# One transfer per weight tile in place of two half transfers, in a four-layer model on one core

## The chip, the core and the metric

The kernel runs on one core of a Trainium2 chip. The metric is the device time of one execution in microseconds (us). The core has a matrix engine (TensorE, PE in the profile, with its weight loads as PEld), three engines for elementwise work (VectorE or DVE, ScalarE or ACT, GpSimd or POOL), a queue engine (SyncE or SP) that here only issues transfers, and 16 DMA engines between the off-chip memory and the on-chip buffer.

## What is computed

Four layers on 512 tokens of width 1024, in float32: a dilated-window attention, a differential attention, then a block with a recurrent mixer, a cross attention to a memory of 256 rows and a squared-ReLU network, and a block with a sliding-window attention, again a cross attention and a squared-ReLU network. Every one is a chain of matrix products with weights, with norms between them:

```python
h = h + rmsnorm(dilated_mixer(rmsnorm(h), dil_w_in, dil_w_out))
h = h + rmsnorm(diff_mixer(rmsnorm(h), diff_w_in, ..., diff_w_out))
for l in range(2):
    h = h + rms_norm(mixer_l(rms_norm(h)))
    h = h + rms_norm(cross_attention(rms_norm(h), mem, w_xq[l], w_xkv[l], w_xo[l]))
    h = h + rms_norm(relu(rms_norm(h) @ w_ff1[l]) ** 2 @ w_ff2[l])
```

## The kernel before

All weights are laid out as 373 tiles of 128 partitions x 1024 float32 (512 KB), in the order in which they are used. A tile passes through four engines, and each works by halves of 512 columns:

- SyncE, `load(n, s)` (lines 344 to 350): brings tile n to `raw[:, s, :]`, s = n % 2, so there are two raw slots. Half h of tile n may overwrite half h of tile n-2, and waits for that: `lo_ready` counts the halves that GpSimd is done with, and the wait is for n*2 + (h-3), that is for half h of tile n-2. Each half is a transfer of its own, with a semaphore of its own (`loaded[s][h]`).
- ScalarE, `split` (lines 1096 to 1102): waits until a slot of the ring `wh` is free (5 slots in the first layer, 4 later: `tile_used` of tile n-5 or n-4) and rounds each half of `raw` to the high part `wh`. It waits for half 0 ahead of the first and for half 1 ahead of the second.
- GpSimd, `rest` (lines 405 to 412): `wl` = `raw` - `wh`, half by half, each counted in `lo_ready`. This is the last reader of the raw half.
- TensorE multiplies: with high and low parts of both operands there are three matmuls for each product (`three`, line 440). Before each half of a tile it waits for `lo_ready`.

ScalarE does its work in a fixed order written out by hand, in which each `split` runs three tiles or so ahead of the tile that TensorE is at. The same engine also evacuates TensorE's banks (`take`, line 1254), and TensorE waits for that (`lin_evac`) before it writes the same bank two tiles later. So a `split` that waits for its load holds up the `take` behind it.

Tiles are not equally long for TensorE. A tile of 24 matmuls of 512 columns is the rule. In the two cross attentions (`cross`, base tile b = 161 for x0 and b = 277 for x1) the tiles are shorter: b to b+7 make the keys of the memory with 24 matmuls of 256 columns each; b+8 to b+15 make its values with 12 matmuls of 512 columns each, with a set of transposes after the first four; then b+16 to b+19 are used with 256 columns for the first half of the tokens, as far as the first half of b+19, then follow transposes (line 474), and only then the rest. ScalarE's order in that stretch is

```python
for m in range(8):
    split_g(b + m + 3)
    take(b + m, xk(m), m % 2, width=MEM)
...
for t in range(TT):
    norm_squares(H, [t], waits=False)
    split_g(b + 11 + t)
half_hi(("g_x_pre", 8 * l), 0, CROSS)
for m in range(15, 20):
    split_g(b + m)
```

`half_hi` (line 1147) is eight evacuations of transposed rows, taken in turns with VectorE. `norm_squares` (lines 1131, 1113, 1114) is the square sum of a block of rows.

Two tiles elsewhere matter below: tile 87, the last one of the first layer's output projection, and tile 275, one of the last of the sliding-window layer's (`out_projection`, tiles 269 to 276). Around both ScalarE has itself issued large loads: a gain row (`gB`, 512 KB) and two blocks of x at tile 87, and `xmem` (1 MB) at tile 275.

Of the kernel before, what the change touches and what calls it, by code (L numbers as in the profile page):

```python
# [67 lines left out]
def build(nc, x, mem, positions, tiles, cols, post, consts, masks, maskd_in, rgw, out, upto="all"):  # L68
    ctx = ExitStack()
    with ctx:  # L70
        def sb(name, shape, dt=F32):
            return ctx.enter_context(nc.sbuf_tensor(name, shape, dt))

        def sem(name):
            return ctx.enter_context(nc.semaphore(name))
# [6 lines left out]
        raw = sb("raw", [P, 2, TILE])  # L82
# [26 lines left out]
        Tps = PS[:, TB0:TB0 + 2, :].rearrange("p b n -> p (b n)")  # L109


        loaded = [[sem(f"half_tile_loaded_{s}_{h}") for h in range(2)] for s in range(2)]
        hi_ready = sem("hi_ready")
        lo_ready = sem("lo_ready")
        tile_used = sem("tile_used")
# [50 lines left out]
        def wait(eng, s, value):  # L166

            if isinstance(value, int) and value <= 0:
                return
            eng.wait_ge(s, value)  # L170
# [15 lines left out]
        def on(name):  # L186
            return upto == "all" or order.index(name) <= order.index(upto)
# [6 lines left out]
        def w_of(part, slot):  # L194
            return part[:, slot, :]
# [12 lines left out]
        def draw(a): return wk(512 * (a % 2))  # L208
        def swp(a): return wk(15360 + 512 * (a % 2))
# [10 lines left out]
        def fraw(a): return wk(512 * (a % 2))  # L220
# [36 lines left out]
        def sraw(a): return wk(512 * (a % 2))  # L257
# [84 lines left out]
        @block.sync  # L342
        def _(sp):
            def load(n, s, again=True):
                src = tiles[n] if isinstance(n, int) else tiles[bass.ds(n, 1)].rearrange("a p n -> (a p) n")
                for h in range(2):
                    hc = slice(512 * h, 512 * h + 512)
                    if again:
                        sp.wait_ge(lo_ready, n * 2 + (h - 3))
                    sp.dma_start(raw[:, s, hc], src[:, hc]).then_inc(loaded[s][h], 16)  # L350

            sp.dma_start(colv[:, :], cols).then_inc(consts_in, 16)
            for t in range(TT):
                sp.dma_start(H[:, t, :], x[t * P:(t + 1) * P, :]).then_inc(x_in[t], 16)
                if t == 0:
                    sp.dma_start(cst[:, :], consts).then_inc(consts_in, 16)
            for s in range(2):
                load(s, s, again=False)
            sp.dma_start(maskn[:, :], masks).then_inc(masks_in, 16)
            sp.dma_start(maskd[:, :], maskd_in.bitcast(BF16)).then_inc(masks_in, 16)  # L360
            sp.dma_start(pos[:, :], positions.partition_broadcast(P)).then_inc(masks_in, 16)
            sp.dma_start(rgw_sb[:, :, :], rgw).then_inc(masks_in, 16)

            def swap_halves(src, a, evac):

                sp.wait_ge(lin_evac, evac)
                for at in range(0, P, 32):
                    to = at ^ 32
                    sp.dma_start(swp(a)[to:to + 32, :], src[at:at + 32, :]).then_inc(halves_swapped[a % 2], 16)

            for n in range(2, 5):
                load(n, n % 2)
            with sp.Fori(0, HP) as i:
                for j in range(10):
                    load(i * 10 + (j + 5), (j + 5) % 2)
                    if j < 6:
                        swap_halves(draw(j), j, i * 10 + (j + 1))
            for n in range(N_D + 5, BASE["diff"] + 5):
                load(n, n % 2)
            with sp.Fori(0, HP) as i:  # L380
                for j in range(4):
                    n = i * 4 + (BASE["diff"] + j + 5)
                    load(n, (BASE["diff"] + j + 5) % 2)
                    if j < 2:
                        swap_halves(fraw(j), j, i * 4 + (LIN["diff"] + j + 1))
            def loads(first, end):

                with sp.Fori(0, (end - first) // 2) as i:
                    for s in range(2):
                        load(i * 2 + (first + s), (first + s) % 2)  # L390
                if (end - first) % 2:
                    load(end - 1, (end - 1) % 2)

            if on("sw"):
                loads(BASE["diff_out"] + 5, BASE["sw"] + 5)
                for m in range(12):
                    load(BASE["sw"] + m + 5, (BASE["sw"] + m + 5) % 2)
                    if m not in (2, 3):
                        swap_halves(sraw(m), m, LIN["sw"] + m + 1)
                loads(BASE["sw"] + 17, n_tiles)  # L400
            else:
                loads(BASE["diff_out"] + 5, n_tiles)
            sp.wait_ge(out_done, 16 * TT)
# [684 lines left out]
        def _(act):  # L1088
# [7 lines left out]
            def split(n, slot, raw_slot, loads, ring, used=None):  # L1096

                wait(act, tile_used, n + (1 - ring) if used is None else used)
                for h in range(2):
                    hc = slice(512 * h, 512 * h + 512)  # L1100
                    act.wait_ge(loaded[raw_slot][h], loads * 16)
                    nc.scalar.activation(w_of(wh, slot)[:, hc], raw[:, raw_slot, hc], ACT.Copy).then_inc(hi_ready, 1)  # L1102

            def split_g(n):

                if n < n_tiles:
                    split(n, slot_of(n), n % 2, n // 2 + 1, G_RING)
# [153 lines left out]
            for n in range(2):  # L1261
                split(n, n, n % 2, n // 2 + 1, D_RING)
            norm_hi(("norm_pre", 0), TT)
            split(2, 2, 0, 2, D_RING)

            def setup():
# [1291 lines left out]
```

## Time and profile before

| | us |
|---|---|
| median of 3 runs | 2483.36 |
| lowest, highest | 2483.32, 2484.29 |
| the profiled execution, its own time | 2485.89 |
| its span, first to last instruction | 2484.1 |
| TensorE busy in the span | 2389.3 (96%) |
| VectorE, ScalarE, GpSimd busy | 1200.3, 1110.6, 1030.5 |

The page of the profile lists an engine's busy time, its idle time with what ended it, and the transfers by line with the time from issue to landing. An "x15" is a count, and "[0.47 <-DMA raw]" behind a row of the timeline says that the engine stood idle 0.47 us before it and what let it go on. A row of the timeline can hold several instructions of the same kind that follow on each other: its two first numbers are then the start of the first and the time to the end of the last.

### The profile page before, as it was taken

Reading aid. Unit: us, or ns where it says so; the run is one execution under the profiler, and the core shown is the slowest. Engines: PE = TensorE matmul, PEld = TensorE weight load, DVE = VectorE, ACT = ScalarE, POOL = GpSimd, SP = SyncE. Lnnn points to the kernel's source line nnn. Section 1 sums busy time; section 2 is a strip of 40 time slices with the busy share of each in tenths; the row PEclk is TensorE's granted clock in tenths of the full one; section 3 lists DMA queues with packets and bytes.
Section 4 is the critical chain, followed back from the end, with each engine's and each line's share of the span. In section 5 each row is a group of like instructions: output and inputs, shape, how many; then the busy total and the mean of one; then the engine's idle time right before and its main releaser. Section 6 shows DMA issues by size and latency. Waiting matters only on the chain.

```text
span 2484.1 us, 40506 instructions
## 1 busy us (share of the span) xinstructions
PE 2389.3 (96%) x13254; PEld 1956.0 (79%) x13254; DVE 1200.3 (48%) x2391; ACT 1110.6 (45%) x2412; POOL 1030.5 (41%) x750
## 2 busy tenths in 40 slices
PE   7999999999999989988999999999898999999998
PEld 6878787877877768666888888887766888888886
DVE  5555455554677762564444522224775424522224
ACT  5433343444555554553644533323565644523332
POOL 4444444442533324432652544443412642544442
PEclk9999999999999999988999999999999999999999
DMA  5333333332332213221431333332322431333332
GB/s 186 114 101 94 102 91 103 101 102 94 105 91 85 85 52 102 71 65 63 127 108 52 95 101 94 96 95 74 90 65 77 132 102 52 111 94 93 101 92 77
DMA packets 126066, 232.01 MB, mean 93 GB/s; under 512 B 17120, under 2 KB 17248, under 8 KB 125920
## 3 DMA queue, kind: packets, MB, share of 16 engines
q1 hardware_dynamic: 123072, 219.56, 29.7%
q10 hardware_dynamic: 2848, 10.49, 1.2%
q8 instruction: 94, 1.54, 0.3%
q14 instruction: 52, 0.43, 0.1%
HBM read 208.48 MB, written 2.10 MB: 85 GB/s over the span
## 4 chain that ended last, share of the span: by engine, by line
issue 53%; PE 24%; POOL 21%; ACT 1%; DVE 1%; POOLq 1%; DMA 0%; ACTq 0%; DVEq 0%; SPq 0%
PE PS L440 22%; POOL wl L411 21%; PE PS L507 1%; PE PS L519 1%; PE PS L474 0%; DMA raw<-tiles_dram 0%; POOLq L410 0%; POOLq L419 0%; ACT wh L1102 0%; DVE H L1781 0%; PE PS L514 0%; ACT work L1211 0%; ACT work L1131 0%; DVE work L1718 0%; ACT work L1254 0%
## 5 line engine op out<-in xcount | busy, mean ns | idle before, releaser
L411 POOL TENSOR_TENSOR wl<-raw,wh 128x512 fp32r<-128x512 f32 x746 | 1030.3, 1404 | 1425.9 <-ACT wh L1102 1424.6
L440 PE MATMUL PS<-uh,wh 128*128 128x512 f32 (+1 forms) x2184 | 810.3, 371 | 13.5 <-ACT work L1254 4.6
L440 PE MATMUL PS<-uh,wl 128*128 128x512 f32 (+1 forms) x2184 | 793.7, 363 | 0.0
L440 PE MATMUL PS<-ul,wh 128*128 128x512 f32 (+1 forms) x2184 | 792.6, 363 | 0.0
L1102 ACT ACTIVATE wh<-raw 128x512 fp32r<-128x512 f32 x746 | 430.5, 623 | 348.3 <-PE PS L440 280.4
L440 PEld LDWEIGHTS PS<-uh,wh 128*128 128x128 f32 x2184 | 414.8, 190 | 99.2 <-issue 15.2
L440 PEld LDWEIGHTS PS<-uh,wl 128*128 128x128 f32 x2184 | 414.2, 190 | 65.1
L440 PEld LDWEIGHTS PS<-ul,wh 128*128 128x128 f32 x2184 | 415.1, 190 | 60.8 <-issue 1.0
L440 PE MATMUL PS<-wh,hid_sb 128*128 128x512 f32 x1024 | 322.1, 396 | 0.0
L1254 ACT ACTIVATE work<-PS 128x512 f32<-128x512 f32 (+1 forms) x156 | 89.7, 575 | 339.6 <-PE PS L440 271.2
L440 PEld LDWEIGHTS PS<-wh,hid_sb 128*128 128x128 f32 x1024 | 192.4, 188 | 46.1
L440 PE MATMUL PS<-wl,hid_sb 128*128 128x512 f32 x512 | 202.5, 395 | 0.0
L440 PE MATMUL PS<-wh,uh 128*128 128x512 f32 x448 | 182.3, 407 | 11.0 <-DVE ul L1771 4.4
L440 PE MATMUL PS<-wl,uh 128*128 128x512 f32 x448 | 177.6, 396 | 0.0
L440 PE MATMUL PS<-wh,ul 128*128 128x512 f32 x448 | 177.6, 396 | 0.0
L507 PE MATMUL PS<-work 64*32 64x128 f32 (+8 forms) x1568 | 141.1, 357 | 14.3 <-DVEq L2174 7.4
L2300 DVE TENSOR_TENSOR work<-work,PS 128x512 f32<-128x512 f32 x96 | 66.0, 687 | 178.1 <-PE PS L440 178.1
L2282 DVE TENSOR_TENSOR work<-work 128x512 f32<-128x512 f32 x64 | 47.5, 743 | 214.4 <-ACT work L1578 214.4
L1235 ACT ACTIVATE work<-work,stat 128x512 f32<-128x512 f32 (+3 forms) x160 | 97.4, 609 | 96.4 <-DVEq L1815 95.1
L440 PEld LDWEIGHTS PS<-wl,hid_sb 128*128 128x128 f32 x512 | 96.3, 188 | 23.2
L440 PEld LDWEIGHTS PS<-wh,uh 128*128 128x128 f32 x448 | 86.1, 192 | 35.7 <-issue 10.3
L507 PEld LDWEIGHTS PS<-work 64*32 64x32 f32 (+2 forms) x1568 | 72.0, 141 | 52.3 <-issue 33.3
(224 smaller groups left out, 2421.6 us busy)
## 6 DMA issues: line engine op xcount, KB each, us to landing
raw<-tiles_dram SPq DMA_DIRECT2D x746, 256.0 KB, 2.7
work<-work SPq DMA_DIRECT2D x296, 64.0 KB, 2.0
gB<-post_dram ACTq DMA_DIRECT2D x8, 512.0 KB, 3.7
H<-x_dram SPq DMA_DIRECT2D x4, 512.0 KB, 6.4
H<-x_dram ACTq DMA_DIRECT2D x4, 512.0 KB, 5.0
work<-mem_dram ACTq DMA_DIRECT2D x2, 1024.0 KB, 5.8
out_dram<-H ACTq DMA_DIRECT2D x4, 512.0 KB, 2.6
cst<-consts_dram SPq DMA_DIRECT2D x1, 644.0 KB, 5.2
```

The lines of the kernel that those rows point to most:

```text
L411: nc.gpsimd.tensor_tensor(w_of(wl, slot)[:, hc], raw[:, s, hc], w_of(wh, slot)[:, hc].bitcast(F32), ALU.subtract).then_inc(lo_ready, 1)
L440: last = nc.tensor.matmul(out, a, b, start=start and m == 0, stop=stop and m == 2)
L507: ins = nc.tensor.matmul(o, q, k, start=first, stop=last)
L519: last = nc.tensor.matmul(out, a, b, start=n == 0, stop=n == len(pairs) - 1)
L1102: nc.scalar.activation(w_of(wh, slot)[:, hc], raw[:, raw_slot, hc], ACT.Copy).then_inc(hi_ready, 1)
L1235: last = nc.scalar.activation(sm, sm, ACT.Exp, bias=bias, scale=-1.0, accum_out=d)
L1254: nc.scalar.activation(dst, PS[:, bank, 0:width], ACT.Copy).then_inc(lin_evac, 1)
L2282: v.tensor_tensor(hs(j), hs(j), hs(j), ALU.mult)
L2300: v.tensor_tensor(ys, ys, PS[:, bk, :], ALU.add).then_inc(y_evac, 1)
```

## The change

The two half transfers become one of 1024 columns with one semaphore for each raw slot. It waits until GpSimd is done with both halves of tile n-2. ScalarE waits once, ahead of the first half. The rounding, the low parts and the matmuls still go by halves.

```diff
-        loaded = [[sem(f"half_tile_loaded_{s}_{h}") for h in range(2)] for s in range(2)]
+        loaded = [sem(f"tile_loaded_{s}") for s in range(2)]
...
             def load(n, s, again=True):
                 src = tiles[n] if isinstance(n, int) else tiles[bass.ds(n, 1)].rearrange("a p n -> (a p) n")
-                for h in range(2):
-                    hc = slice(512 * h, 512 * h + 512)
-                    if again:
-                        sp.wait_ge(lo_ready, n * 2 + (h - 3))
-                    sp.dma_start(raw[:, s, hc], src[:, hc]).then_inc(loaded[s][h], 16)
+                if again:
+                    sp.wait_ge(lo_ready, n * 2 - 2)
+                sp.dma_start(raw[:, s, :], src[:, :]).then_inc(loaded[s], 16)
...
                 wait(act, tile_used, n + (1 - ring) if used is None else used)
+                act.wait_ge(loaded[raw_slot], loads * 16)
                 for h in range(2):
                     hc = slice(512 * h, 512 * h + 512)
-                    act.wait_ge(loaded[raw_slot][h], loads * 16)
                     nc.scalar.activation(w_of(wh, slot)[:, hc], raw[:, raw_slot, hc], ACT.Copy).then_inc(hi_ready, 1)
```

## Rows read from the trace of the kernel before

**Rows 1.** The page: span, busy times, and DMA issues (count, KB, us to landing).
```profile
span 2484.1 us, 40506 instructions
...
PE 2389.3 (96%) x13254; PEld 1956.0 (79%) x13254; DVE 1200.3 (48%) x2391; ACT 1110.6 (45%) x2412; POOL 1030.5 (41%) x750
...
raw<-tiles_dram SPq DMA_DIRECT2D x746, 256.0 KB, 2.7
```

**Rows 2.** The waits of the whole span: who <- for whom, us, times, longest.
```profile
ACT wh L1102 <- DMA raw<-tiles_dram: 49.6, 48, 5.1
...
PE PS L440 <- POOL wl L411: 7.1, 4, 3.3
```

**Rows 3.** The waits between 1200 and 1285 us, then between 1940 and 2020 us.
```profile
ACT wh L1102 <- DMA raw<-tiles_dram: 17.0, 20, 4.2
...
ACT wh L1102 <- DMA raw<-tiles_dram: 18.6, 19, 2.6
```

**Rows 4.** Timeline of ScalarE, x0: start us, us, what [idle before <-releaser].
```profile
1209.13 1.21 ACT L1102 ACTIVATE wh<-raw 128x512 fp32r<-128x512 f32 x2 [4.17 <-DMA raw<-tiles_dram]
...
1238.05 1.18 ACT L1102 ACTIVATE wh<-raw 128x512 fp32r<-128x512 f32 x2 [0.16 <-issue]
1239.13 0.82 ACT L1147 ACTIVATE uh<-PS,colv 128x256 fp32r<-128x256 f32 x2
...
1241.95 0.87 ACT L1147 ACTIVATE uh<-PS,colv 128x256 fp32r<-128x256 f32 x2 [0.21 <-DVE ul L1737]
```

**Rows 5.** Timeline of GpSimd in x0, from tile 164's second half on.
```profile
1207.97 1.25 POOL L411 TENSOR_TENSOR wl<-raw,wh 128x512 fp32r<-128x512 f32 x1
...
1209.84 10.18 POOL L411 TENSOR_TENSOR wl<-raw,wh 128x512 fp32r<-128x512 f32 x8 [0.62 <-ACT wh L1102]
```

**Rows 6.** The transfers' queue at 1212.5 us: the second half of tile 167.
```profile
1212.55 0.33 SPq L350 DMA_DIRECT2D raw<-tiles_dram x1
```

**Rows 7.** `gB` alone, 512 KB in one transfer, 905 to 911 us: time to landing.
```profile
DMA to landing us min/median/max: 3.3/3.3/3.3
```

**Rows 8.** GpSimd's group between 1229 and 1249 us (busy, mean ns | idle before).
```profile
L411 POOL TENSOR_TENSOR wl<-raw,wh 128x512 fp32r<-128x512 f32 x12 | 16.9, 1441 | 3.9 <-ACT wh L1102 3.9
```

**Rows 9.** Timeline of GpSimd in x1: the two halves of tile 280.
```profile
1948.43 2.30 POOL L411 TENSOR_TENSOR wl<-raw,wh 128x512 fp32r<-128x512 f32 x1
...
1950.69 1.27 POOL L411 TENSOR_TENSOR wl<-raw,wh 128x512 fp32r<-128x512 f32 x1
```

**Rows 10.** Timeline of TensorE: first matmuls of tiles 177, 293; transposes behind 180, 296.
```profile
1250.21 0.28 PE L440 MATMUL PS<-uh,wh 128*128 128x256 f32 x1
...
1260.28 1.69 PE L474 MATMUL PS<-cst,work 128*128 128x128 f32 x14
...
1991.34 0.28 PE L440 MATMUL PS<-uh,wh 128*128 128x256 f32 x1
...
2001.41 1.36 PE L474 MATMUL PS<-cst,work 128*128 128x128 f32 x11
```

**Rows 11.** ScalarE at tile 87; TensorE's wait between 617 and 624 us.
```profile
603.80 1.24 ACT L1102 ACTIVATE wh<-raw 128x512 fp32r<-128x512 f32 x2 [5.11 <-DMA raw<-tiles_dram]
...
PE PS L474 <- DVE work L1718: 2.4, 1, 2.4
```

**Rows 12.** Tile 275: ScalarE's first and second half, then TensorE.
```profile
1916.04 0.63 ACT L1102 ACTIVATE wh<-raw 128x512 fp32r<-128x512 f32 x1 [3.44 <-DMA raw<-tiles_dram]
...
1918.94 0.63 ACT L1102 ACTIVATE wh<-raw 128x512 fp32r<-128x512 f32 x1 [2.27 <-DMA raw<-tiles_dram]
...
1920.99 0.50 PE L440 MATMUL PS<-wh,uh 128*128 128x512 f32 x1 [0.39 <-POOL wl L411]
```

**Rows 13.** TensorE in x0 and x1 at a pause; then clock and load of 1211 to 1215.
```profile
1210.66 0.39 PE L440 MATMUL PS<-uh,wh 128*128 128x256 f32 x1 [2.50 <-ACT work L1254]
...
1952.37 0.39 PE L440 MATMUL PS<-uh,wh 128*128 128x256 f32 x1 [1.49 <-ACT work L1254]
...
1211.00:1215.00 4.00, 4.00 (x23) 4.00 (x22) 0.00 (x0) 2.16 (x4) 4.00 (x5) 0.57 0.67 193
```

## The prediction, made before the kernel was changed

> **What bounds the kernel now.** I read the page first: TensorE is busy for 2389.3 of 2484.1 us, and every other engine for less than half [rows 1]. So a change in the supply of weights costs or gives only what it does to TensorE's idle time. The loads have plenty of time on average: 746 halves land 2.7 us after their issue. The waits say where they don't: ScalarE waited for a load 48 times, 49.6 us in all, and TensorE for the low parts 7.1 us in 4 waits [rows 2]. By stretch, 39 of the 48 waits and 35.6 of the 49.6 us lie in two of 80 us each, the cross attentions x0 and x1 [rows 3]. Elsewhere a tile is 24 matmuls of 512 columns, twice the 0.12 us of those of 256 columns [rows 10], so some 5.8 us, and ScalarE hardly ever waits for one.
>
> **What the change takes away.** 373 issues on SyncE and as many waits on ScalarE. SyncE's queue is waiting anyway, and a half's issue takes 0.33 us beside its own wait [rows 6]; I cost this at nothing. The swaps of halves that stand behind a load in that queue were held by the same last wait (second half of tile n-2) before, so they are issued no later.
>
> **What it adds.** The first half is now asked for when the second half of tile n-2 is done, one GpSimd operation (1.27 us) later; it lands with the whole tile; and GpSimd can't begin before. Where ScalarE comes to a tile long after it landed, that is hidden. In x0 and x1 it is not, so I work out the loop there. From GpSimd's end of a tile to its end of the tile that follows in the same raw slot:
> - to the issue: the first two of the eight operations end at 1209.84 + 2.54 = 1212.38 [rows 5], the issue is at 1212.55 [rows 6]: 0.17.
> - to the landing: no transfer of 512 KB on this line exists. `gB` of the same size took 3.3 alone [rows 7]. Not below the half's 2.7 [rows 1]. `gB` shows 0.6 for the second 256 KB; if that costs half as much again beside other traffic, 3.6 (an estimate), the upper end. I take 3.3, the nearest row.
> - ScalarE to GpSimd: 1209.84 - 1209.13 = 0.71 [rows 4, 5].
> - two halves on GpSimd: 10.18 / 8 = 1.27 each, 2.54 [rows 5].
>
> Sum 6.72 us for two tiles (there are two slots), 3.36 a tile. Before, the first half's load ran beside GpSimd's second half, and GpSimd itself was the limit: 2.54 a tile. What TensorE wants: 84 matmuls lie between 1250.21 and 1260.28, so 0.12 each, and tile 180 begins 12 of them ahead of the transposes, at 1258.84; tile 296 at 2001.41 - 1.44 = 1999.97 [rows 10]. Tile 164 began at 1210.66 and tile 280 at 1952.37 [rows 13]: 16 tiles in 48.2 and 47.6 us, 3.0 a tile. So supply is faster than demand before (2.54 against 3.0) and slower after (3.36), and the lead melts away within the stretch.
>
> *x0.* Tile 164 is done at 1207.97 + 1.25 = 1209.22 [rows 5]. Eight loops on is tile 180, its first half one operation earlier: 1209.22 + 53.76 - 1.27 = 1261.71, which is 2.87 after 1258.84. Two things come on top, since the loop now has no room. GpSimd's operations take 1.44 instead of 1.27 between 1229 and 1249 [rows 8]: 0.34 a tile, three tiles of this slot, 1.0. And ScalarE does `half_hi` between tile 175 and tile 176, from 1239.13 to 1242.82, 3.7 us [rows 4]. Tile 165 lands no earlier than before (its second half was split at 1209.13 + 1.21 - 0.63 = 1209.71), is done at 1209.7 + 3.25 = 1212.95, tile 173 at 1212.95 + 4 x 6.72 + 0.34 = 1240.2; tile 175 lands 3.47 later, its two halves take ScalarE 1.15, `half_hi` 3.7: 1248.5. Tile 176 has then landed since 1209.22 + 5 x 6.72 + 0.68 + 3.47 = 1247.0: 1.5 more. x0: 5.4 us.
>
> *x1.* Tile 280 is done at 1950.69 + 1.27 = 1951.96, tile 279 at 1948.5 [rows 9]. Tile 296: 1951.96 + 53.76 - 1.27 = 2004.45, 4.48 after 1999.97. Slow operations as in x0, 1.0. `half_hi`: tile 289 done at 1948.5 + 33.6 + 0.34 = 1982.4, plus 3.47, 1.15 and 3.7 is 1990.8; tile 292 landed at 1951.96 + 33.6 + 0.34 + 3.47 = 1989.4: 1.4. x1: 6.9 us. In both the `take` behind a waiting `split` adds pauses earlier in the stretch (as at 1952.37, a pause of 1.49 which grows by about 1.0 [rows 13]); they don't add to the end, which supply sets. After tile 180 or 296 TensorE has the second half of the tokens to do with tiles that are there, and nothing makes good what it lost: it is the bound.
>
> *Tile 87.* ScalarE waited 5.11 for the first half [rows 11], behind its own large loads, and its squares, the norm and TensorE's pause of 2.4 follow from there. It began the second half at 603.80 + 1.24 - 0.63 = 604.41, so that had landed at most 0.6 later; the whole lands with it: bounds 0 and 1.0, I take 0.6. *Tile 275.* TensorE waited 0.39 for its second low part; ScalarE had the first half at 1916.04 and the second at 1918.94 [rows 12]. If the whole lands at 1918.9, both halves then pass GpSimd in turn and it ends 1.27 later. If it has a better share beside `xmem` than the two halves had, it lands up to 2 us sooner, and the 0.4 pause is gone. Bounds -0.4 and +1.3; I take +0.8, nearer to the landing that the row shows.
>
> Sum: 5.4 + 6.9 + 0.6 + 0.8 = 13.7 us. On the profiled execution's 2485.89 that gives 2499.6; on the median of 2483.36, 2.5 lower, 2497.0.
>
> **A rule against this.** The rows show a half landing in 2.7 us and 512 KB in 3.3 [rows 1, 7], so most of a transfer is a fixed part. The Trainium skill (page "DMA: Bandwidth & Descriptors", section "Anatomy of one DMA — SWDGE (gpsimd) path") puts it as 2.0 us and bytes / 436e3 for GpSimd's own path: 2.6 for a half, 3.2 for a whole, an estimate that agrees with the rows within 0.1; by 3.2 the loop is 0.1 shorter and the sum 1.6 smaller. The same page, "Rules for kernel authors", advises few and large transfers, which here would mean a gain. The first rival below is what such a gain would be in this kernel.
>
> **The rivals.**
> - *Faster: one fixed part instead of two.* Where the DMA engines are full, at tiles 87 and 275, one request could come through sooner than two. The most it can give is TensorE's pause of 0.4 and part of the 2.4 [rows 11, 12], 1.5 together, if at the same time x0 and x1 cost nothing: 2481.9. Against it: the two halves were in flight side by side, so their fixed parts overlapped. To be faster by over 0.2% it would have to give 5 us. Chance 0.03.
> - *No difference: the lead holds.* If a whole lands as fast as a half, in 2.7, the loop is 6.12, tile 180 is ready at 1209.22 + 48.96 - 1.27 = 1256.9, 1.9 early, and the slow operations eat half of that; tile 296 at 1999.65 + 1.0, 0.7 late, and up to 1.3 for `half_hi`. With tiles 87 and 275 that is 1 to 4 us: 2486. It decides at a landing of about 3.0. For it: a half's 2.7 is mostly not moving of data. Against it: the 3.3 of `gB`. Chance 0.13.
> - *Slower still: the clock.* After TensorE's pause of 2.5 in x0 the granted clock was 0.57 between 1211 and 1215 [rows 13], the lower level of 1.2 GHz for most of 4 us. More and longer pauses could bring this three or four times more, 1.7 us each where supply doesn't hide it, and with a landing of 3.6 (the loop 0.3 longer, 8 loops, two stretches: 4.8) the time is 2504. Chance 0.20.
> - The forecast, 2490 to 2501: chance 0.64.
>
> **How the numbers follow.** About 0.2% (5 us) is what a measurement of this kernel can tell from no change. Forecast and clock rival are slower by more; of the second rival nearly all is within: faster 0.03, same 0.13, slower 0.84. Range for 8 in 10: from the middle of the second rival's upper part, 2487, to beyond the clock's 2504, 2506.
>
> **What would show it.** Landing of the 373 transfers at a median of 3.2 to 3.4. In x0 and x1 GpSimd with gaps ended by ScalarE at each tile, ScalarE's waits for loads together some 30 us more, and TensorE with some 12 us more of idle time, in waits for low parts and for `take`. Everywhere else no new wait. Wrong it would be if TensorE's idle time grew in the first two layers or in the squared-ReLU networks (then the loads have less room than I read), or if x0 and x1 kept their length.

## The result, and the profile after the change

| | before, in the same comparison | changed |
|---|---|---|
| median, us | 2483.36 (5 runs) | 2502.3 (5 runs) |
| lowest, highest | 2482.56, 2486.25 | 2494.5, 2504.91 |
| the profiled execution, its own time | 2485.89 | 2504.91 |
| its span | 2484.1 | 2503.1 |

The ratio is 1.0067, with a 95% interval of 1.0049 to 1.0085: 0.67% slower, which is 16.6 us; the two medians lie 18.9 us apart. The forecast was 13.6 slower, in a range of 3.6 to 22.6. The profiled execution of the changed kernel is the slowest of its five, so what its trace adds up to is a little more than the median.

The page of the changed kernel (busy time of the engines; then DMA issues with KB of each and the median us from issue to landing):

```profile
span 2503.1 us, 39095 instructions
...
PE 2395.7 (96%) x13254; PEld 1957.8 (78%) x13254; DVE 1192.9 (48%) x2391; ACT 1109.0 (44%) x2412; POOL 1029.9 (41%) x750
...
raw<-tiles_dram SPq DMA_DIRECT2D x373, 512.0 KB, 3.6
```

The span is 19.0 us longer than in [rows 1] and TensorE's busy time 6.4 longer, for the same 13254 matmuls; so 12.6 of the 19.0 are idle time. A tile lands after 3.6 us where a half took 2.7.

The waits of the whole span (who <- for whom: us in all, times, longest), to be held against [rows 2]:

```profile
ACT wh L1100 <- DMA raw<-tiles_dram: 97.1, 52, 6.7
...
PE PS L438 <- POOL wl L409: 16.0, 16, 3.3
```

ScalarE's waits for loads grew by 47.5 us, TensorE's for low parts by 8.9. And by stretch, against [rows 3], first between 1200 and 1300 us, then between 1940 and 2040:

```profile
ACT wh L1100 <- DMA raw<-tiles_dram: 34.0, 17, 4.5
...
PE PS L438 <- POOL wl L409: 3.7, 5, 1.1
...
PE PS L438 <- ACT work L1252: 3.7, 3, 2.8
...
ACT wh L1100 <- DMA raw<-tiles_dram: 32.9, 17, 4.4
...
PE PS L438 <- POOL wl L409: 3.9, 7, 1.0
...
PE PS L438 <- ACT work L1252: 3.4, 2, 2.7
```

TensorE's only wait of these two kinds in the same stretches before was that for a `take` (1200 to 1285, then 1940 to 2020 us):

```profile
PE PS L440 <- ACT work L1254: 2.5, 1, 2.5
...
PE PS L440 <- ACT work L1254: 2.1, 2, 1.5
```

So TensorE's waits in the two crosses went from 4.6 us to 14.7. That is 10.1 of the 12.6 us of idle time.

The length of a run is TensorE's, so I took the time at which TensorE finished each tile in both traces and subtracted before from after. This difference is called the shift. The table shows what it gained in each stretch, in us:

| where | shift gained there |
|---|---|
| start, to tile 83 | -0.9 |
| tile 87 | +0.65 |
| tiles 139, 140 | +2.9 |
| tiles 164 to 180 (x0) | +7.05 |
| tile 185 | -1.6 |
| tiles 257 to 269, up and down | -1.8 |
| tiles 272 to 276 | +3.1 |
| tiles 280 to 296 (x1) | +9.3 |
| tiles 297 to the end | 0 |

The small steps between these add up to 0.5. Within the long stretches of full tiles, the first network (193 to 256) and the second one after 297, the shift doesn't move at all.

Tiles 139 and 140 lost nothing to the supply. The window from 1000 to 1030 us, before and after (columns: length; busy time of PE, PEld, DVE, ACT, POOL with the number of instructions; TensorE's granted clock; DMA share; GB/s):

```profile
1000.00:1030.00 30.00, 25.73 (x87) 17.51 (x86) 20.52 (x25) 13.65 (x21) 11.09 (x8) 0.89 0.22 66
```

```profile
1000.00:1030.00 30.00, 25.73 (x74) 16.64 (x73) 20.50 (x25) 11.02 (x17) 10.54 (x7) 0.77 0.24 70
```

TensorE is busy for the same 25.73 us but does 74 matmuls in place of 87: the granted clock was 0.77 against 0.89. In the changed kernel's execution the two stays at the lower level (1.2 GHz), around 1005 and around 1019, lasted 6.8 us each, in that of before 3.4. No run here gives this a cause in the change. In the profiles of the experiments below the same two tiles gained 2.9, 2.8 and 2.6 (whole in the crosses, halves in the crosses, rows of 2 KB), nothing (late request, both waited for, third slot with halves) and -0.8 (third slot with whole transfers, `xmem` later): it comes and goes with halves and with whole tiles. The -1.6 at tile 185 is the same thing the other way round: TensorE's idle time in tiles 181 to 185 is 4.45 us in both kernels, and only its busy time differs.

The 3.1 at tiles 272 to 276 has two parts. TensorE waited for the second low part of tile 275 for 1.87 us (first line), where it was 0.39 before [rows 12]. And behind this pause the granted clock was 0.57 (second line): TensorE did 13 matmuls in 4 us. Before, behind the short pause, it was 1.00, with 19 matmuls in 4 us (second fence):

```profile
1929.09 0.50 PE L438 MATMUL PS<-wh,uh 128*128 128x512 f32 x1 [1.87 <-POOL wl L409]
...
1930.00:1934.00 4.00, 4.00 (x13) 3.08 (x12) 2.23 (x8) 3.61 (x10) 1.51 (x2) 0.57 0.73 213
```

```profile
1922.00:1926.00 4.00, 4.00 (x19) 3.30 (x18) 1.71 (x6) 3.71 (x8) 1.45 (x2) 1.00 0.64 192
```

So 1.5 us are the later low part, and the other 1.6 the lower clock behind the pause.

### The profile page after: what moved, and what is told of

The parts are those of the page before. It is cut to its first block, busy times and chain, and to the rows that moved or that the text cites. A ratio compares the mean times of both kernels' runs of the same rounds, so it can differ in the third digit from the quotient of the medians.

```text
span 2503.1 us, 39095 instructions
## 1 busy us (share of the span) xinstructions
PE 2395.7 (96%) x13254; PEld 1957.8 (78%) x13254; DVE 1192.9 (48%) x2391; ACT 1109.0 (44%) x2412; POOL 1029.9 (41%) x750
## 4 chain that ended last, share of the span: by engine, by line
issue 45%; PE 31%; POOL 19%; DVE 2%; ACT 1%; POOLq 1%; DMA 0%; ACTq 0%; DVEq 0%; SPq 0%
PE PS L438 27%; POOL wl L409 19%; PE PS L505 1%; PE PS L517 1%; PE PS L472 1%; PE PS L512 0%; DMA raw<-tiles_dram 0%; POOLq L408 0%; DVE H L1779 0%; ACT work L1209 0%; POOLq L417 0%; ACT work L1129 0%; ACT wh L1100 0%; PE PS L771 0%; DVE work L1812 0%
```

## The loop in the two cross attentions

The timeline of ScalarE in x0 (start us, duration, what, idle time before it and what ended it), against [rows 4]:

```profile
1215.78 1.15 ACT L1100 ACTIVATE wh<-raw 128x512 fp32r<-128x512 f32 x2 [1.84 <-DMA raw<-tiles_dram]
1216.83 0.36 ACT L1252 ACTIVATE work<-PS 128x256 f32<-128x256 f32 x1
1219.63 1.15 ACT L1100 ACTIVATE wh<-raw 128x512 fp32r<-128x512 f32 x2 [2.44 <-DMA raw<-tiles_dram]
1222.92 1.15 ACT L1100 ACTIVATE wh<-raw 128x512 fp32r<-128x512 f32 x2 [1.87 <-DMA raw<-tiles_dram]
```

Every `split` waits for its load, and the distance from one to the next is 3.85 and 3.29 us, 7.14 for the two raw slots. Tile 164 to tile 180 took 48.2 us before, 3.0 a tile [rows 13]. GpSimd between 1205 and 1275 us (operations, busy us, mean ns | idle time before, and who ended it):

```profile
L409 POOL TENSOR_TENSOR wl<-raw,wh 128x512 fp32r<-128x512 f32 x36 | 47.9, 1354 | 22.9 <-ACT wh L1100 22.9
```

Its gaps are all ended by ScalarE. And TensorE (the first three lines wait for a low part in x0; the fourth is the transposes behind tile 180, which began at 1260.28 before [rows 10]; the last is in x1 and waits 2.68 for a `take`):

```profile
1254.17 0.50 PE L438 MATMUL PS<-wh,uh 128*128 128x512 f32 x1 [1.01 <-POOL wl L409]
1255.85 0.50 PE L438 MATMUL PS<-wh,uh 128*128 128x512 f32 x1 [0.72 <-POOL wl L409]
...
1268.80 0.39 PE L438 MATMUL PS<-uh,wh 128*128 128x256 f32 x1 [1.07 <-POOL wl L409]
1270.34 1.91 PE L472 MATMUL PS<-cst,work 128*128 128x128 f32 x16
...
1963.27 0.39 PE L438 MATMUL PS<-uh,wh 128*128 128x256 f32 x1 [2.68 <-ACT work L1252]
```

Taken apart, as means over tiles 167 to 180 and 283 to 296 of the changed kernel, the loop of one raw slot is:

| | worked out | x0 | x1 |
|---|---|---|---|
| GpSimd's end to the issue | 0.17 | 0.16 | 0.16 |
| issue to landing | 3.3 | 3.48 | 3.66 |
| landing to ScalarE's start | 0 | 0.19 | 0.10 |
| ScalarE's start to GpSimd's second end | 3.25 | 3.39 | 3.39 |
| sum | 6.72 | 7.21 | 7.31 |
| before, measured | | 6.06 | 6.03 |

The last two steps hold the slow GpSimd operations and `half_hi`, which the prediction added apart. The loop of before is that of TensorE's demand, 3.0 a tile, and not its own limit.

These loops account for the end of both stretches. GpSimd was done with tile 164 at 1212.22 and with tile 280 at 1961.64. Eight loops later, less one operation of 1.27, is 1268.6 and 2018.9, and there TensorE began tiles 180 and 296 behind a wait for just this low part: at 1268.80 (the fence above) and at 2018.86. A granted clock of 0.57 behind the pause of 2.68 in x1 (1964 to 1968 us) therefore cost nothing on top: TensorE still had to wait for the supply at the end.

The landings of the loads in the two stretches, 1218 to 1262 and 1965 to 2018 us:

```profile
DMA to landing us min/median/max: 3.2/3.4/3.6
...
DMA to landing us min/median/max: 3.4/3.6/4.1
```

## The experiments

My theory was that the change costs time only in the two crosses, since there the loop over two raw slots (request, landing, ScalarE, two halves on GpSimd) becomes longer than TensorE's demand, and it does so by three things, the later request, the wait for both halves and the longer landing of 512 KB. Rivals: that one of the three does it alone; that the changed transfers cost time elsewhere, at tiles 87 and 275 and by the clock; that the number or the size of the pieces makes the transfer slow. The first four ran side by side, beside a median of 2484.11 of the kernel before (20 runs, 2476.57 to 2487.81), the last four beside 2484.19 (21 runs, 2476.3 to 2487.97). "x0" to "rest" are shifts of the profiled execution against that of the kernel before, read as in the table above. "Loop" is the mean time from GpSimd's end of tile n-2 to its end of tile n, also where there are three slots.

| | median | ratio (95%) | x0 | x1 | tile 87 | tile 275 | rest | loop, x0 / x1 |
|---|---|---|---|---|---|---|---|---|
| the change | 2502.3 | 1.0067 (1.0049, 1.0085) | 7.0 | 9.3 | 0.65 | 3.1 | -1.1 | 7.21 / 7.31 |
| late request | 2491.21 | 1.0031 (1.0021, 1.0041) | 2.6 | 4.3 | -0.2 | -0.5 | -4.0 | 6.72 / 6.77 |
| both waited for | 2493.62 | 1.0035 (1.0022, 1.0048) | 2.8 | 5.1 | 0.6 | 1.3 | 0.2 | 6.70 / 6.85 |
| whole in the crosses | 2498.05 | 1.0057 (1.0044, 1.0070) | 6.6 | 8.6 | -1.3 | -0.7 | -1.0 | |
| halves in the crosses | 2483.01 | 1.0000 (0.9989, 1.0011) | -0.1 | -0.3 | 0.4 | -0.2 | -2.7 | |
| third slot, whole | 2479.32 | 0.9986 (0.9977, 0.9995) | -3.4 | -2.1 | 0.6 | 0.3 | -9.2 | 5.72 / 5.66 |
| third slot, halves | 2478.83 | 0.9988 (0.9976, 0.9999) | -4.0 | -1.7 | 0.8 | -0.7 | -3.5 | |
| `xmem` later | 2499.52 | 1.0065 (1.0050, 1.0080) | 7.5 | 10.1 | 0.9 | -0.7 | -7.2 | |
| rows of 2 KB | 2506.53 | 1.0089 (1.0073, 1.0104) | 10.5 | 12.6 | 0.9 | 0.7 | -0.6 | 7.70 / 7.68 |

**e1_late_request.** The kernel before, with two transfers and two semaphores, but the first half too is asked for only when the second half of tile n-2 is done:

```diff
                     if again:
-                        sp.wait_ge(lo_ready, n * 2 + (h - 3))
+                        sp.wait_ge(lo_ready, n * 2 - 2)
```

> Two half transfers with a semaphore each, as before; both are asked for only when both halves of tile n-2 are done. Theory of the loop: issue 0.17, a half lands in 2.7, ScalarE to GpSimd 0.71, two halves on GpSimd 2.54: 6.1 to 6.3 us for two tiles instead of 7.0, about 3.1 a tile against the 3.0 that TensorE wants, so 2 to 5 us slower than before, nearly all in the two cross attentions, and median landing of a half 2.7 to 3.0. Rival (the loss of 19 us comes from asking late): nearly all of it, 13 to 19 us, appears here already. Rival (it comes from the size of the transfer): no difference to before, 0 to 1.

Measured: 7.1 us slower, more than the 2 to 5 expected, and the loop 6.72 and 6.77 instead of 6.1 to 6.3. The waits between 1200 and 1275 us:

```profile
ACT wh L1102 <- DMA raw<-tiles_dram: 23.8, 16, 4.4
...
PE PS L440 <- ACT work L1254: 2.2, 1, 2.2
PE PS L440 <- POOL wl L411: 1.4, 2, 0.7
```

So the late request by itself, with first halves that land after 2.75 us, turns the surplus of the supply into a shortage. Single loops of this run are 6.2 to 6.3 (GpSimd ended tiles 170, 172 and 174 at 1226.56, 1232.88 and 1239.05), as 0.17 + 2.75 + 3.25 = 6.17 gives. The mean is higher through single events: one half that landed after 4.49, and `half_hi` together with slow GpSimd operations ahead of tile 176 (8.5 from 174 to 176).

**e2_both_waited.** Two transfers, asked for as before, but ScalarE waits for both before it begins:

```diff
                 for h in range(2):
-                    hc = slice(512 * h, 512 * h + 512)
                     act.wait_ge(loaded[raw_slot][h], loads * 16)
+                for h in range(2):
+                    hc = slice(512 * h, 512 * h + 512)
                     nc.scalar.activation(w_of(wh, slot)[:, hc], raw[:, raw_slot, hc], ACT.Copy).then_inc(hi_ready, 1)
```

> Two half transfers, each asked for as before when its own half of tile n-2 is done; ScalarE waits for both before it begins the first half. Theory of the loop: issue 0.17, second half lands in 2.85, 0.71, 2.54: 6.3 us for two tiles, 3 to 7 us slower than before, in the cross attentions. Rival (size of the transfer alone): 0 to 1. If this one and the one with the late request cost the same, the landing of the second half is what both wait for.

Measured: 9.5 us slower, above the 3 to 7 expected, the loop 6.70 and 6.85. It is nearly the loop of the late request. In both kernels the half that ScalarE has to wait for is asked for 0.17 us after GpSimd's second operation on tile n-2: there the first half (it lands after 2.75), here the second (after 2.89). The two parts are one loss, counted once: the overlap of a load with GpSimd's second half. That both together, with halves, lose no more than one follows from this working and was not run.

**e3_whole_in_crosses and e4_halves_in_crosses.** Tiles 165 to 180 and 281 to 296 are treated in the other way than the rest. In the first they come whole and all others in halves; in the second they come in halves and the other 341 whole. (The loads of these tiles are written out on SyncE instead of looped, with semaphores of their own.)

```diff
-                for h in range(2):
-                    hc = slice(512 * h, 512 * h + 512)
-                    if again:
-                        sp.wait_ge(lo_ready, n * 2 + (h - 3))
-                    sp.dma_start(raw[:, s, hc], src[:, hc]).then_inc(loaded[s][h], 16)
+                sems = other[s] if is_other(n) else loaded[s]
+                whole = len(sems) == 1
+                for h in range(len(sems)):
+                    hc = slice(0, 1024) if whole else slice(512 * h, 512 * h + 512)
+                    if former is not None:
+                        sp.wait_ge(lo_ready, former * 2 + (2 if whole else h + 1))
+                    sp.dma_start(raw[:, s, hc], src[:, hc]).then_inc(sems[h], 16)
```

> Whole transfers for tiles 165 to 180 and 281 to 296 alone, halves elsewhere. Theory of the loop: 14 to 17 us slower than before, the shift of TensorE against before is zero up to tile 164, 7 at tile 180, and 16 at tile 296. Rival (the loss is spread over all tiles, the swaps of halves and the clock): 1 to 4.

> The reverse: halves for tiles 165 to 180 and 281 to 296, whole transfers for the other 341. Theory: 1 to 5 us slower than before, 3 of it at tile 275 and 0.6 at tile 87, nothing in the cross attentions. Rival (spread loss): 12 to 18 slower. If changes of the clock are behind part of the 19, this one moves by up to 3 either way between tiles 123 and 153 and from 185 to 272.

Measured: 32 whole tiles in the crosses cost 13.9 us (14 to 17 were expected), 341 whole tiles elsewhere nothing (1.1 less than before, the interval of the ratio on both sides of 1; 1 to 5 more were expected, above all at tile 275). That settles the place. The two together come to 0.57% where the whole change has 0.67%; the intervals overlap widely, so the runs don't show whether anything is missing between them.

In the second, whole tiles land after 3.58 us as in the changed kernel, and the waits in x0 (1200 to 1285 us) are as many as before [rows 3] and 5.7 us longer on ScalarE, while TensorE's one wait for `take` is the 2.5 of [rows 13]:

```profile
ACT wh L1136 <- DMA raw<-tiles_dram: 22.7, 20, 4.2
...
PE PS L470 <- ACT work L1288: 2.5, 1, 2.5
```

That kernel also has the whole tile at 275, beside `xmem`, and lost nothing there (-0.2).

**e5_third_slot_whole and e6_third_slot_halves.** If the loop over two slots is the cause, a third slot must take the loss away with the transfer left whole. `raw` gets a third slot, used in the two stretches alone, and a load there waits for tile n-3 (GpSimd's loop is written out around them too):

```diff
-        raw = sb("raw", [P, 2, TILE])
+        raw = sb("raw", [P, 3, TILE])
...
+        def raw_of(n):
+            if True and is_other(n):
+                return next((2, 1, 0)[(n - a) % 3] for a, b in OTHER if a <= n < b)
+            return n % 2
```

The first has whole transfers everywhere, the second halves everywhere.

> Whole transfers for all tiles, but a third raw slot takes part for tiles 165 to 180 and 281 to 296, so that tile n waits for tile n-3 there. Theory of the loop: 7.0 us now serve three tiles, 2.3 a tile, under GpSimd's own 2.54 and TensorE's 3.0: x0 and x1 lose nothing against before, 2481 to 2487. Rival (a longer transfer disturbs the engines or the DMA engines): still 10 or more slower, whatever the number of slots.

> Half transfers everywhere, a third raw slot for the same 32 tiles. In the kernel before ScalarE still waited 35 us for loads in x0 and x1, and TensorE 4 us for a bank behind such a wait (1210.66 and 1952.37). Theory: these pauses shrink, 1 to 4 us faster than before. Rival (GpSimd's 2.54 was enough): the same as before within 1.

Measured: 4.9 and 5.4 us faster than the kernel before by the medians (expected: a time of 2481 to 2487 for the first, where 2479.32 was measured, and 1 to 4 faster for the second). By the ratios it is 0.14% and 0.12%, whose intervals end just under 1. The changed kernel is 0.67% above the same kernel before, so a third slot takes the whole loss away with the transfers left whole; whole or halves makes no difference that can be told. That the gain on the kernel before is more than noise rests on the traces: the crosses are 5.5 and 5.7 shorter. What a third slot takes from the kernel before are TensorE's waits of 2.5 us in x0 and 2.1 in x1, in which a `take` stood behind a `split` that waited for its load, and the clock behind the first of them: there it was 0.57 between 1211 and 1215 [rows 13], and TensorE's busy time from tile 164 to 180 was 64.8 us against 63.5 and 63.2 with three slots. The same place with three slots and halves, with 44 matmuls in 5 us:

```profile
1210.00:1215.00 5.00, 5.00 (x44) 5.00 (x44) 0.00 (x0) 3.03 (x6) 5.00 (x5) 1.00 0.73 206
```

The waits of the version with whole tiles between 1190 and 1285 us:

```profile
ACT wh L1143 <- DMA raw<-tiles_dram: 20.6, 11, 3.7
...
PE PS L477 <- ACT work L1295: 0.4, 1, 0.4
```

ScalarE still waits for loads, but TensorE's wait behind it is 0.4 where it was 2.5. So the two raw slots were a limit of the kernel before already, though a small one. (GpSimd's loop is written out in this kernel as well, and no run separates that; its operations, not its issues, fill its time, 1.29 us each in the median.)

Of the 13.7 us by which that profiled execution is shorter, 9.2 lie outside the crosses and the two tiles. I put them down to the clock and count no gain: the mean granted clock (here the kernel with three slots, the kernel before and the changed one) was high in this one execution, and the median of its 11 runs is only 4.9 below.

```profile
core 0: 2470.4 us, clock 0.987
```

```profile
core 0: 2484.1 us, clock 0.982
```

```profile
core 0: 2503.1 us, clock 0.980
```

**e7_xmem_later.** The changed kernel, with the 1 MB load `xmem` issued by ScalarE after the high parts of tile 275 instead of ahead of them. It asks whether the 3.1 at tiles 272 to 276 came from the whole tile that lands beside it.

```diff
-                if mem_of is not None:
+                late = mem_of is not None and begun
+                if mem_of is not None and not late:
                     act.dma_start(xmem, mem.rearrange("(t p) n -> p t n", p=P)).then_inc(mem_in, 16)
...
                     split_g(b + j + 3)
+                    if late and j == 3:
+                        act.dma_start(xmem, mem.rearrange("(t p) n -> p t n", p=P)).then_inc(mem_in, 16)
```

What the profiles of the changed kernel and of the kernel with the move show of ScalarE there:

```profile
1925.82 2.38 ACT L1100 ACTIVATE wh<-raw 128x512 fp32r<-128x512 f32 x4 [6.61 <-DMA raw<-tiles_dram]
```

```profile
1916.59 0.63 ACT L1100 ACTIVATE wh<-raw 128x512 fp32r<-128x512 f32 x1 [3.49 <-DMA raw<-tiles_dram]
1916.64 0.39 ACTq L1200 DMA_DIRECT2D work<-mem_dram  x1
```

> The changed kernel, with ScalarE's load of the memory rows in front of x1 issued behind the split of tile 275 instead of ahead of it. Theory: tile 275 then lands in 3.3 to 3.6 instead of 6.8 and the 3 us lost between tiles 272 and 276 are back, unless the norm of the memory rows, now 6 us later, holds up x1's first tile. Rival (275 is late since its request is late, not since its landing is long): no change.

Measured: the tile landed after 3.7 us, as the theory has it, and tiles 272 to 276 gained 0.7 instead of losing 3.1. But x1 lost 10.1 instead of 9.3, and the ratio of 1.0065 is that of the change, 1.0067, within the intervals: by the runs the rival's "no change" can't be told from a gain of 3. In the changed kernel's profiled execution the tile landed 6.8 us after its issue; in the kernel with halves in the crosses, as whole and beside the same `xmem`, after 5.1, and there nothing was lost:

```profile
1908.51 0.39 ACTq L1228 DMA_DIRECT2D work<-mem_dram  x1
...
1915.08 1.16 ACT L1136 ACTIVATE wh<-raw 128x512 fp32r<-128x512 f32 x2 [4.90 <-DMA raw<-tiles_dram]
```

With three slots and in the kernel with rows of 2 KB it landed beside `xmem` too, after 5.6 and 6.1 us, and tiles 272 to 276 lost 0.3 and 0.7. So the 3.1 is what this collision cost in one execution, half of it by the clock behind the pause, and not a steady price of the change. How often it comes, with one profile for each kernel, stays open.

**e8_rows_of_2kb.** One transfer with one semaphore, as in the change, but `raw` is laid out so that a partition's 4 KB fall into two pieces of 2 KB (ScalarE's and GpSimd's reads of `raw` follow the new layout and are left out here):

```diff
-        raw = sb("raw", [P, 2, TILE])
+        raw = sb("raw", [P, 2, 2, TILE // 2])
...
-                sp.dma_start(raw[:, s, :], src[:, :]).then_inc(loaded[s], 16)
+                sp.dma_start(raw[:, :, s, :], src[:, :].rearrange("p (h c) -> p h c", h=2)).then_inc(loaded[s], 16)
```

> One transfer a tile with one semaphore as in the changed kernel, but the two halves of a raw slot lie apart, so each row of 4 KB arrives as two of 2 KB. If the landing of 3.6 us comes from the number of bytes it stays at 3.5 to 3.7 and the time at 2495 to 2505; if it comes from the longer rows it is near 3.3, and the time some 5 us lower; if from the number of pieces it grows to 4 or more, with 10 us on top.

Measured: 2506.53, 22.3 above the kernel before, and the landing 4.0. So it is the pieces (at equal bytes their number and their length can't be told apart), but with less than the expected 10 us on top of the change: the medians differ by 4.2, the crosses by 6.8.

```profile
raw<-tiles_dram SPq DMA_DIRECT2D x373, 512.0 KB, 4.0
...
q1 hardware_dynamic: 117104, 219.53, 29.7%
```

```profile
q1 hardware_dynamic: 69360, 219.53, 29.0%
```

The second fence is the same line for the change (packets, MB, share of the engines' time). The same bytes come in 47,744 more packets. A tile in 256 pieces lands 0.45 to 0.5 later than in 128, and the loop grows by 0.49 and 0.37, the crosses by 3.5 and 3.3. Eight loops by these give 3.9 and 3.0. This is the same sum as in the prediction, made with another landing, and it comes out.

**What the runs make of the loss.** In the crosses the change costs 16.3 us in its profiled execution. Waiting for both halves, at a half's landing, costs 7.9 of them; the loop from there to the change is 0.51 and 0.46 longer, times eight 4.1 and 3.7, against 4.2 and 4.2 measured (7.0 - 2.8, 9.3 - 5.1). So about half is the lost overlap, and half the longer landing of the larger transfer. This is the split in this order, overlap first: a longer landing with the overlap kept was not run.

## Why the prediction was right, and where it was off

- *What bounds the kernel.* Right. 12.6 of the 19.0 went into TensorE's idle time (some 12 was forecast), 10.1 of them into waits in the two crosses, and neither squared-ReLU network lost anything.
- *What is taken away costs and gives nothing.* This was right as far as the runs tell: with 341 whole tiles outside the crosses the ratio was 1.0000, with an interval of 0.0011 on either side.
- *The loop in x0 and x1.* This was right in mechanism. The term that was mis-sized is the landing: 3.3 was taken from `gB` [rows 7], with an upper end of 3.6, and 3.48 and 3.66 were measured in the stretches. With these the sum grows by eight times 0.18 and 0.36, 1.4 and 2.9: 5.4 + 1.4 = 6.8 and 6.9 + 2.9 = 9.8, against 7.0 and 9.3. The other steps, the issue (0.16 for 0.17) and ScalarE and GpSimd (3.39 with the slow operations, 3.25 without), held. The upper end of 3.6, "half as much again beside other traffic", gave the right number, but not for its reason: of the 373 whole tiles, the 189 that landed with no other transfer in flight took 3.5 too. The better row was on the page of the kernel before: `gB` is loaded eight times, 3.3 is the shortest landing of the eight, and their median is 3.7:

```profile
gB<-post_dram ACTq DMA_DIRECT2D x8, 512.0 KB, 3.7
```

- *A rule beside it.* A transfer of 512 KB on this queue takes 3.55 us in the median, and a half of 256 KB, always beside its other half, 2.7. The Trainium skill (page "DMA: Bandwidth & Descriptors", section "Anatomy of one DMA — SWDGE (gpsimd) path") gives an estimate of 3.2 and 2.6 by its 2.0 us and bytes / 436e3, for GpSimd's path; for 512 KB on SyncE's the measurement is 0.35 higher, and it decides. That page's advice for few and large transfers ("Rules for kernel authors") is meant for bandwidth and for transfers under 64 KB. Here neither was the limit (the queue took 29% of the DMA engines' time), and one transfer in place of two cost 0.67%.
- *The rival of a lead that holds* was to decide at a landing of about 3.0. It falls, since the landing was 3.55, and the late request shows that it was too kind: with first halves at 2.75 the kernel still lost 7.1 us, where the rival had 1 to 4 for a landing of 2.7. The step that failed there is the lead. The rival reckoned with a loop of 6.12 throughout, and the measured mean was 6.7: one late landing of 4.49 or a `half_hi` is not made good afterwards when the loop and the demand are nearly equal.
- *Tile 87.* 0.6 forecast, +0.65 measured. In the other profiles the same place gave -1.3 to +0.9, so the agreement is in part luck.
- *Tile 275.* 0.8 forecast, bounds -0.4 and +1.3; +3.1 measured, outside of them. The landing is not what failed: the whole landed 6.8 us after its issue, and the second half before, asked for at the same point, after 6.6. As the prediction has it, GpSimd was done one operation later, and TensorE's pause grew by 1.5. The step that failed is what follows from a pause: 1.6 more went to the granted clock of 0.57 behind it, for which the sum has no term (the rival of the clock had 1.7 for each such pause). In three other kernels with a whole tile there beside `xmem` it was -0.2, 0.3 and 0.7, within the bounds.
- *ScalarE's waits.* In x0 and x1 they grew from 35.6 to 66.9 us, by 31 where some 30 was forecast. But "everywhere else no new wait" was wrong: over the whole span they grew by 47.5. The other 16 us lie outside the crosses; there, tile 275 apart, TensorE waited no longer for low parts than before. A wait of ScalarE costs time only through the `take` or the low part behind it.
- *The clock.* The median of 2502.3 lies in the stated range but above the 2490 to 2501 of the forecast, and nearer to the rival's 2504 than to 2497. The first of the rival's two reasons held, the landing of 3.6. The second, lower clock behind longer pauses, held once where it cost time, the 1.6 us at tile 275; in x1 it came too and was hidden behind the supply. The 2.9 us at tiles 139 and 140 are of the lower level as well, but nothing had changed there, and the granted clock over the whole was 0.980 against 0.982.
- *Missed altogether:* that the kernel before also lost time to its two raw slots, 3 to 5 us. The prediction had the pauses and the lower clock behind one of them [rows 13] and used them only as a sign of what would grow.

## What to carry to other kernels

Before you merge two transfers into one, look at what the halves let you do early: here a half was asked for while the other half's buffer was still read, and in the stretches where the loop of request, landing and use is about as long as the demand, merged transfers cost 0.57%, and elsewhere nothing that could be told from noise. Work out that loop for each number of buffers, with the landing of a transfer of the new size from many rows and its spread, not from one. If the loop is the limit, one more buffer in just those stretches is worth more than the form of the transfer: it took the kernel from 0.67% above the old one to 0.14% below. And count a pause of TensorE with what comes behind it: in the profiled execution a pause that grew by 1.5 us was followed by a stretch at the lower clock that cost as much again.

## What was not expected of the hardware

- From 256 KB to 512 KB on this queue, with 128 pieces each, the median time to landing goes from 2.7 to 3.55 us. In the packets of 512 KB alone in flight (medians of 189) the first piece of data moves 0.96 us after the issue, the last ends at 3.2 and the semaphore is up at 3.5. A piece of 4 KB takes 159 ns of a DMA engine, one of 2 KB in the kernel before 84 ns. The number of pieces has a price too: 0.45 to 0.5 us for 128 more at equal bytes. Most of it comes ahead of the data: with 256 pieces the first one moves 1.33 us after the issue.
- Small transfers behind the tiles on SyncE's queue got slower with them: the swaps of 64 KB went from 2.0 to 2.9 us (first line of the fence: the page of the changed kernel). No stretch outside the crosses lost time by it (the ratio with halves in the crosses alone is 1.0000).

```profile
work<-work SPq DMA_DIRECT2D x296, 64.0 KB, 2.9
```

- The kernel before alone ranges over 11 us in 20 runs on one chip (2476.57 to 2487.81), and the profiled executions of all kernels over a mean granted clock of 0.980 to 0.987. A shift of a few us in one profiled execution, without a wait beside it, says nothing of a change.
